# Three joints of a decoder stack: last output job, eviction, square, statistic, root, residual and first tile by halves of the tokens

## What is computed

```
for i in range(DEPTH_2):
    a = rms_norm_2(h, pre_mix_norm[i])
    m = hgrn2_mixer(...) if i == 0 else mla_mixer(...)     # ends in "@ w_out"
    h = h + rms_norm_2(m, post_mix_norm[i])                # joints "hg_post", "mla_post"
    f = squared_relu_mlp(rms_norm_2(h, pre_mlp_norm[i]), w_mlp_in[i], w_mlp_out[i])
    h = h + rms_norm_2(f, post_mlp_norm[i])
    e = p[i] @ w_ple_proj[i]
    g = sigmoid(h @ w_ple_gate[i])
    h = h + rms_norm_2(g * e, ple_norm[i])                 # joint "ple0_post" for i = 0
```

## Time and profile before

| | |
|---|---|
| median of 3 runs (lowest, highest) | 2754.61 us (2754.1, 2755.46) |
| the profiled execution: time, span | 2754.22 us, 2752.4 us |
| busy: PE, DVE, ACT, POOL | 2680.1, 1367.5, 1213.1, 1071.2 us |
| instructions: PE, DVE, ACT, POOL | 13878, 2435, 1883, 803 |
| mean granted TensorE clock | 0.994 |

### The profile page before, as it was taken

The page is one execution under the profiler, slowest core; times in us unless marked ns, Lnnn a source line. Parts: engine busy times, 40 slices in busy tenths (PEclk is TensorE's granted clock), DMA queues, the critical chain, the costliest instruction groups (busy, mean ns, idle before and its releaser), DMA issues.

```text
span 2752.4 us, 41868 instructions
## 1 busy us (share of the span) xinstructions
PE 2680.1 (97%) x13878; PEld 2137.5 (78%) x13878; DVE 1367.5 (50%) x2435; ACT 1213.1 (44%) x1883; POOL 1071.2 (39%) x803
## 2 busy tenths in 40 slices
PE   7999999999999999999999999999999999999999
PEld 6887777767777777778887788887677877788886
DVE  7335333676666567676755321128753353321126
ACT  5224433544444455565544432235554463433234
POOL 5544333423233333443344444444412213444442
PEclk9999999999999999999999999999999999999999
DMA  4332222211121221222223333333211202333331
GB/s 160 96 96 81 83 72 72 69 54 55 37 61 44 70 69 61 78 76 69 69 69 92 92 96 95 93 109 92 77 39 41 66 31 69 99 93 97 93 107 54
DMA packets 59641, 211.87 MB, mean 77 GB/s; under 512 B 6688, under 2 KB 7072, under 8 KB 59552
## 3 DMA queue, kind: packets, MB, share of 16 engines
q1 hardware_dynamic: 57744, 206.89, 24.6%
q10 hardware_dynamic: 1520, 2.75, 0.3%
q0 software_dynamic: 288, 1.05, 0.1%
HBM read 208.57 MB, written 2.10 MB: 77 GB/s over the span
## 4 chain that ended last, share of the span: by engine, by line
issue 36%; PE 23%; POOL 17%; DVE 2%; POOLq 0%; ACT 0%; DVEq 0%
POOL weights_low L374 17%; PE bank L1323 6%; PE bank L1325 6%; PE bank L1324 6%; PE bank L1427 2%; PE bank L1409 0%; PE bank L1450 0%; PE bank L1434 0%; DVE work L1761 0%; PE bank L1535 0%; DVE activations_low L454 0%; PE bank L1516 0%; PE bank L1540 0%; PE bank L1512 0%; DVE residual L2374 0%
## 5 line engine op out<-in xcount | busy, mean ns | idle before, releaser
L374 POOL TENSOR_TENSOR weights_low<-weights_raw,weights_high 128x512 fp32r<-128x512 f32 x776 | 1042.3, 1366 | 1539.4 <-ACT weights_high L358 1520.6
L1323 PE MATMUL bank<-activations_high,weights_high 128*128 128x512 f32 x2912 | 1184.4, 407 | 38.5 <-POOL weights_low L374 16.8
L1325 PE MATMUL bank<-activations_high,weights_low 128*128 128x512 f32 x2912 | 1141.4, 392 | 0.0
L1324 PE MATMUL bank<-activations_low,weights_high 128*128 128x512 f32 x2912 | 1140.6, 392 | 0.0
L1323 PEld LDWEIGHTS bank<-activations_high,weights_high 128*128 128x128 f32 x2912 | 550.0, 189 | 176.2 <-issue 20.1
L1325 PEld LDWEIGHTS bank<-activations_high,weights_low 128*128 128x128 f32 x2912 | 549.5, 189 | 117.2
L1324 PEld LDWEIGHTS bank<-activations_low,weights_high 128*128 128x128 f32 x2912 | 550.8, 189 | 110.0 <-issue 8.4
L358 ACT ACTIVATE weights_high<-weights_raw 128x1024 fp32r<-128x1024 f32 x384 | 404.0, 1053 | 302.3 <-PE bank L1325 294.8
L2864 DVE TENSOR_TENSOR mixed<-bank,mixed 128x512 f32 (+1 forms) x48 | 33.2, 692 | 193.9 <-PE bank L1325 193.9
L2808 ACT ACTIVATE to_split<-work 128x512 f32<-128x512 f32 x64 | 40.5, 632 | 184.0 <-DVE work L2850 184.0
L2850 DVE SCALAR_TENSOR_TENSOR work<-bank,rstd 128x512 f32<-128x512 f32 x64 | 44.2, 690 | 144.4 <-PE bank L1325 138.6
(11 more groups left out here) (452 smaller groups left out, 3272.9 us busy)
## 6 DMA issues: line engine op xcount, KB each, us to landing
weights_raw<-weights SPq DMA_DIRECT2D x388, 512.0 KB, 3.6
out_t<-residual SPq DMA_DIRECT2D x8, 256.0 KB, 2.1
residual<-x_t ACTq DMA_DIRECT2D x2, 512.0 KB, 7.1
residual<-x_t POOLq DMA_DIRECT2D x2, 512.0 KB, 9.9
work<-p_t ACTq DMA_DIRECT2D x2, 512.0 KB, 4.2
const<-consts SPq DMA_DIRECT2D x1, 713.0 KB, 12.6
const<-consts SPq DMA_DIRECT2D x1, 321.0 KB, 11.5
root<-positions ACTq DMA_DIRECT2D x1, 256.0 KB, 3.1
```

Of the source, the lines that this page charges most:

```text
L374: K.nc.gpsimd.tensor_tensor(K.w_lo[:, s, part], K.raw[:, s, part], K.w_hi[:, s, part].bitcast(F32), ALU.subtract).then_inc(K.job_sems["low ...
L1323: K.nc.tensor.matmul(dst, wh, K.act_hi[:, t, :], start=k == 0, stop=False)
L1324: K.nc.tensor.matmul(dst, wh, K.act_lo[:, t, :], start=False, stop=False)
L1325: ins = K.nc.tensor.matmul(dst, wl, K.act_hi[:, t, :], start=False, stop=k == len(tiles) - 1)
```

## The change

At the three joints, the eighth job of the output phase and what follows it up to the first tile of the next phase are cut in two halves of 256 tokens (`COLUMNS`).

* PE (`joint_pe`): 24 matmuls of 128x256 for the first half into bank 6, then 24 for the second into the job's own bank. Between the second half's matmuls stand the statistic's matmuls, also in halves (banks 7 and 5): the sum of six before its first tile, the square of tile 6 before its third, the first half of the square of tile 7 before its sixth; the second half of it comes after the job. Two filling matmuls end it, where there were one and four.
* DVE and ACT evict, square, take the root of and add half after half, with a semaphore `joint` of 7 steps a joint. The square of tile 7 is now DVE's in all three (`joint_square`); in `hg_out` and `mla_outb` it was ACT's.
* The last `weight_high` ahead, which waits for the eighth job, is moved: between the two roots in `hg` and `mla`, behind the first tile's high part in `ple0`.
* The first high and low part of the next activations are made in halves; the low part of tile 0 is now made before tile 1 is begun.

```diff
+def joint_pe(e, stage, c, tiles):
+    K, s, (n, _) = e.K, c % SLOTS, STAT_SIZE[stage]
+    last, mm, ones = FIRST_SQUARE[stage] + n - 1, e.K.nc.tensor.matmul, e.K.c("ones")[:, 0:P]
+    def piece(k, half):
+        t, cut, dst = tiles[k], COLUMNS[half], joint_bank(e, c, half)
+        wh, wl = K.w_hi[:, s, k * P:(k + 1) * P], K.w_lo[:, s, k * P:(k + 1) * P]
+        mm(dst, wh, K.act_hi[:, t, cut], start=k == 0, stop=False)
+        mm(dst, wh, K.act_lo[:, t, cut], start=False, stop=False)
+        return mm(dst, wl, K.act_hi[:, t, cut], start=False, stop=k == DT - 1)
+    def summed(half, src, start=False, stop=False):
+        cut = COLUMNS[half]
+        return mm(K.ps[JOINT_STAT_BANKS[half]][:, cut], ones, src[:, cut], start=start, stop=stop)
+    job_start(e, c, None, 1)
+    for k in range(DT):
+        if k == DT // 2:
+            second_half(e, c)
+        ins = piece(k, 0)
+    joint_signal(e, ins)
+    e.eng.wait_ge(K.sem("rstd_ready"), STAT_NO[stage])
+    e.eng.wait_ge(K.sem("square_used"), last - 1)
+    for half in range(2):
+        ins = summed(half, K.root, True)
+    ins.then_inc(K.sem("sum_ready"), 1)
+    for k in range(DT):
+        if k == 2:
+            e.eng.wait_ge(K.sem("square_ready"), last)
+            for half in range(2):
+                ins = summed(half, K.sq[:, (last - 1) % 2, :])
+            ins.then_inc(K.sem("square_used"), 1)
+        if k == 5:
+            joint_wait(e, stage, 3)
+            joint_signal(e, summed(0, K.sq[:, last % 2, :], False, True))
+        ins = piece(k, 1)
+    ins.then_inc(K.job_sems["done"], 1)
+    e.eng.wait_ge(K.sem("square_ready"), last + 1)
+    summed(1, K.sq[:, last % 2, :], False, True).then_inc(K.sem("square_used"), 1)
...
 def ahead_act(e, phase, done=0):
...
-            if n == DT - 1:
-                weight_high(e, c0 + DT + AHEAD)
-            square_tile(e, SUMMED_BY[phase], 0, n)
+            if n < DT - 1:
+                square_tile(e, stage, 0, n)
+        joint_root(e, stage, 0)
+        weight_high(e, c0 + DT + AHEAD)
+        joint_root(e, stage, 1)
...
+def post_act(e, step, split, tile0=0, col=None, squares=None, weight=None):
...
+    if joint:
+        joint_wait(e, step + "_post", 6)
+        joint_signal(e, K.nc.scalar.activation(K.act_hi[:, tile0, COLUMNS[0]], K.X[:, 0, COLUMNS[0]], ACT.Copy, scale=col(0)))
     for k in range(DT):
+        cut = COLUMNS[1] if joint and k == 0 else slice(0, S)
         e.eng.wait_ge(K.sem("x_ready"), X_DONE[step] - DT + k + 1)
...
+        if weight and k == 0:
+            weight_high(e, weight)
         if squares:
             square_of(e, squares, k, K.X[:, k, :])
...
+    if joint:
+        for half, cut in enumerate(COLUMNS):
+            if half == 0:
+                joint_wait(e, stage, 5)
+            else:
+                stat_vector(e, stage)
+            e.steps.step(v.scalar_tensor_tensor(K.M[:, 0, cut], K.M[:, 0, cut], K.col(weight, col0), K.rstd[:, cut],
+                                                ALU.mult, ALU.mult))
+            e.steps.wait()
+            ins = v.tensor_tensor(K.X[:, 0, cut], K.X[:, 0, cut], K.M[:, 0, cut], ALU.add)
+            if half == 0:
+                joint_signal(e, ins)
+            else:
+                ins.then_inc(K.sem("x_ready"), 1)
+        joint_wait(e, stage, 7)
+        low_first(COLUMNS[0])
+        e.eng.wait_ge(K.sem("split_high_done"), FIRST_SPLIT[split] + 1)
+        low_first(COLUMNS[1]).then_inc(K.sem("split_done"), 1)
...
 def ple_act(e, name, layer):
...
+        last = gate + DT - 1
+        joint_wait(e, name + "_post", 1)
+        joint_signal(e, act(K.M[:, DT - 1, COLUMNS[0]], joint_bank(e, last, 0), ACT.Sigmoid))
+        square(DT - 2)
+        job_wait(e, last)
+        act(K.M[:, DT - 1, COLUMNS[1]], joint_bank(e, last, 1), ACT.Sigmoid).then_inc(K.job_sems["bank"][last % SLOTS], 1)
+        K.nc.scalar.preload_act_table_set("natural_log_exp_and_others")
+        for half in range(2):
+            joint_root(e, name + "_post", half)
```

More of the change, by code:

```diff
@@ new lines, in joint_square, with joint_root @@
+def joint_square(e, stage, half):
+    K, last = e.K, FIRST_SQUARE[stage] + DT - 1
+    src, cut = K.M[:, DT - 1, :], COLUMNS[half]
+    ins = K.nc.vector.scalar_tensor_tensor(K.sq[:, last % 2, cut], src[:, cut], 1.0 / D, src[:, cut], ALU.mult, ALU.mult)
+    if half == 0:
+        joint_signal(e, ins)
+    else:
+        ins.then_inc(K.sem("square_ready"), 1)
+def joint_root(e, stage, half):
+    K, cut = e.K, COLUMNS[half]
+    if half == 0:
+        joint_wait(e, stage, 4)
+    else:
+        e.eng.wait_ge(K.sem("square_used"), FIRST_SQUARE[stage] + DT)
+    ins = inverse_root(e, K.rstd[:, cut], K.root[:, cut], K.ps[JOINT_STAT_BANKS[half]][:, cut])
+    if half == 0:
+        joint_signal(e, ins)
+    else:
+        ins.then_inc(K.sem("rstd_ready"), 1)
@@ L710, in out_pe, with out_joint_pe @@
                 job(e, c0 + r, i, tiles)
+def out_joint_pe(e, phase, split, stage, tiles=B_TILES, skip=0):
+    c0 = FIRST_JOB[phase]
+    job_with_waits(e, c0, None, tiles, split, skip)
+    for n in range(1, DT - 1):
+        job(e, c0 + n, None, tiles)
+    joint_pe(e, stage, c0 + DT - 1, tiles)
+    keep_busy(e, 2)
 HELD = DT - 1
@@ L2310, in out_m_dve, with evicted @@
         e.steps.wait()
-    if phase == "hg_out":
-        for n in range(DT):
+    if phase in SUMMED_BY:
+        stage, v = SUMMED_BY[phase], K.nc.vector
+        def evicted(n, half=None):
+            if half is None:
+                m, bank = K.M[:, n, :], bank_of(e, c0 + n)[:, :]
+            else:
+                m, bank = K.M[:, n, COLUMNS[half]], joint_bank(e, c0 + n, half)
+            return v.tensor_tensor(m, bank, m, ALU.add) if add else v.tensor_copy(m, bank)
+        for n in range(DT - 1):
             job_wait(e, c0 + n)
-            K.nc.vector.tensor_copy(K.M[:, n, :], bank_of(e, c0 + n)[:, :]).then_inc(count, 1)
+            evicted(n).then_inc(count, 1)
             e.eng.wait_ge(count, base + n + 1)
@@ L2484, in hg_pe @@
         job(e, c0 + r)
[L2485 to L2486 removed]
+    out_joint_pe(e, "hg_out", "hg_y", "hg_post")
 def hg_act(e):
@@ L2949, in ple_pe @@
     quad_by_halves(e, gate, name + "_h", B_TILES)
-    for r in range(4, DT):
+    for r in range(4, DT if nth else DT - 1):
         job(e, gate + r, None, B_TILES)
+    if not nth:
+        for use in ("e5", "e6", "e7"):
+            ring.wait_read(use, nth)
+        joint_pe(e, name + "_post", gate + DT - 1, B_TILES)
+        keep_busy(e, 2)
+        return
     ring.wait_read("e6", nth)
-    if not nth:
-        stat_tensor(e, name + "_post")
-        return
     for use in ("e5", "e7"):
@@ L2988, in square @@
         square_of(e, name + "_post", n, K.M[:, n, :])
-    for n in range(DT):
+    for n in range(DT if nth else DT - 1):
         job_wait(e, gate + n)
@@ L3163, in mla_pe @@
                 mla_pair_pe(e, b, ring, ident, trip, c, i, s)
-        out_pe(e, out, "mla_y", A_TILES, part * DT)
-    stat_tensor(e, "mla_post")
+        if part:
+            out_joint_pe(e, out, "mla_y", "mla_post", A_TILES, DT)
+        else:
+            out_pe(e, out, "mla_y", A_TILES)
 def mla_values(e, c, bank, first):
```

96 lines of the change are left out of this document (68 added, 28 removed).

## The result

| | before | after |
|---|---|---|
| median of runs, us | 2755.03 (2754.1 to 2757.08, 6 runs) | 2766.42 (2764.64 to 2768.3, 6 runs) |
| span of the profiled execution, us | 2752.4 | 2762.8 |
| mean granted clock | 0.994 | 0.992 |

A forecast was written before the change was run, and what follows sets the result against it. PE's waits for one chain at three joints, 26.4 us together, were taken as the most that can be won. Losses of 1.4 (hg, mla), 5.2 (ple0) and 3.2 (clock), 9.8 on 2754.22, gave 2764.0, range 2757 to 2769.

The forecast's parts named there:

- case A: All three joints: the forecast itself, 9.8 us slower, 2764.0 us; chance 0.5.
- case D: Joints: all four idle times and a second one in a row lose clock, with slow forms; 14 us, 2768; chance 0.15.
- hg and mla, the chain: PE resumes at T+14.1 (T: eighth job's first matmul), 0.5 us later than now, because POOL's instructions hold up DVE.
- hg and mla, the tiles behind: PE waits 0.2 us at tile 1, nothing more lost later; with the chain 0.7 us a joint, 1.4 together.
- ple0, the sum of six: PE idles 3.6 us mid-job for the late sum of six; resumes at T+17.7, 2.85 us later than before.
- ple0, tile 1: DVE, held up by POOL, ends tile 1's low part 5.2 us behind tile 0's; PE stops 2.3 us.
- a wait of over 2 us: Sign in ple0: PE waits over 2 us for tile 1's low part, with DVE instructions of 1.1 to 1.8 beside POOL.
- The clock: Behind four new idle times at the joints, two falls to half clock at 1.6 us each: 3.2 us, bounds 0 and 6.4.
- The sum: Whole kernel: 1.4 at hg and mla, 5.2 at ple0, 3.2 for the clock, 9.8 us slower.
- B: Clock stays up or falls once, or POOL slips between DVE's at hg and mla: 6.6 or 4.6 us, 2759 to 2762; chance 0.25.
- C's turning point: ple0: whether the sum of six is in `K.root` by T+2.9, 3.6 us earlier than the trace has it.
- C: Joints: the halves overlap as they are laid out; -1.4 us, 2752.8 us; chance 0.1.

The follow-up runs named there:

- experiment 5: Changed kernel, but at hg and mla the last weights' high part stands behind tile 0's high part, as in ple0: 2768.64 us, ratio 1.0049 to before.
- Experiment 3: Changed kernel plus four fillers before ple0's wait for the sum of six, and four instead of two behind each joint: 2764.35 us, ratio 1.0035 to before.
- experiment 9: Changed kernel with last job whole, tile 0 whole, four fillers, weights' high part ahead of the roots; halves only for eviction, square, statistic, root: 2753.2 us, ratio 0.9994.
- Experiment 4: Changed kernel, but in ple0 the second half's 24 matmuls directly follow the first's, with both halves' sums behind them: 2759.2 us, ratio 1.0015 to before.
- experiment 6: Experiment 4's kernel, with ple0's last weights' high part moved back before the table load: 2758.23 us, ratio 1.0014 to before.
- experiment 7: Experiment 6's kernel with four fillers instead of two behind each joint: 2756.47 us, ratio 1.0006 to before.
- experiments 1: Changed kernel with ple0_post as before, only hg_post and mla_post by halves: 2759.19 us, ratio 1.0019 to before.

## Why the prediction was right, and where it was not

The forecast was 2764.0 in a range of 2757 to 2769; the median is 2766.4. The mechanisms at the three joints are those of case A, named as likeliest; only the number of falls of the clock is that of case D. Step by step:

- **hg and mla, the chain.** Right. T+14.1 was forecast, T+13.87 measured; without POOL T+13.1 was forecast, and experiment 5 gave T+12.89. DVE's add and multiply beside POOL take 1.37 and 1.46. The first is 0.42 plus most of what POOL's first instruction had left (with 1.30 us for it, 1500.12 + 1.30 - 1500.38 = 1.04, of which 0.95 is seen). Of the two, only the multiply's 0.98 moved PE, as forecast.
- **hg and mla, the tiles behind.** This is the term that failed. I had "PE waits 0.2" and "nothing more is lost". Experiment 3 shows 0.3 at tile 1 and 0.5 at the last tile, 0.8 in all where the sum had 0.2; with the 0.3 by which PE resumes later (0.5 in the sum) that is 1.1 a joint where the sum had 0.7. The step was that each later tile takes DVE 2.53 and PE 2.72, so that PE, once stopped at tile 1, never meets DVE again. By that PE would reach the last tile 19 us behind the resumption. It does so after 17.13 in before and 17.14 in experiment 9, because `raw_quad` does not have four jobs take every tile in turn: it does so for the first six tiles (`EARLY` is `DT - 2`), and then the first job alone takes tile 6, 3 matmuls, and comes to tile 7. That is 75 matmuls instead of 84, and in both traces PE makes 75 steps from the one to the other. DVE was just in time there already. Its pace of 2.53 holds in experiment 3, so the 0.8 by which tile 1 is late stays to the end, and PE pays the rest of it at the last tile.
- **ple0, the sum of six.** Right. PE's wait is 3.47 where 3.6 was forecast, the resumption at full clock T+17.51 (experiment 3) where it was T+17.7. In after the second half of the job is late by 1.3 more (T+13.2 where T+11.93 was forecast), which is the half clock. Experiment 4 takes the wait out of the job, and PE resumes 5.75 earlier than in after: 2.64 that were lost against before, 1.84 that the halves behind the job now win, and 1.3 of clock.
- **ple0, tile 1.** Right in mechanism, but the sign did not show. Tile 1's low part ends 5.1 behind tile 0's (5.2 forecast). The wait for it is 2.10 where nothing hides it (2.3 forecast), and experiment 6 removes it by moving the weights' parts ahead. In after only 0.49 of it is seen, where I had named a wait of over 2 us as a sign, since half clock in tile 0 fills the rest: the stall and the fall were added up and in fact overlapped.
- **The clock.** The sum had two falls at 1.6, 3.2 in all; there are four at the joints, and they cost less each. At hg and mla one is worth 0.74 and 0.77 (after against experiment 3). At ple0 the one behind the sum's wait moves the resumption by 18.78 - 17.51 = 1.3. For ple0 without any fall there is only an estimate: experiment 3 resumes 4.48 later than experiment 4 and costs 5.58 more, so its fall behind tile 1's wait cost 1.10, and without it ple0 would be at 5.5. The clock is then 1.3 of the 6.74, and 2.8 at the three joints together. That this is near 3.2 is luck: twice the falls at less than half the price. The error was to add the clock to the tile waits as if they were apart: a slow PE and a PE that waits for DVE lose the same microseconds.
- **The sum.** 9.8 was forecast for the profiled execution and 10.4 found. Without the clock 6.6 was forecast, and 1.09 + 5.5 + 1.11 = 7.7 is what the traces give, with the estimate above in it; the clock's 2.8 instead of 3.2 takes some of the difference back. The stretches outside the joints, +1.6 and -1.6, cancel by chance.
- **The rivals.** B asked for the clock to stay up: it did not stay up, and with the falls gone at hg and mla (experiment 3) the kernel is still at 2764.35. B's 4.6 also needed POOL to slip between DVE's instructions, and POOL met them. D had all four idle times followed by a fall, at 14 us. Four falls are there, one of them behind the 1.79 at ple0 instead of the forecast stall, and the median lies between A's 2764 and D's 2768; D's price of 1.6 for each fall was too high. C's turning point was right in kind: with the sum of six out of the way (experiments 4, 6 and 7) ple0 resumes 1.8 earlier than before, and once POOL is moved its price is -1.06 (experiment 7; in experiment 6, with a fall of the clock behind the joint, it is -0.24).

The Trainium skill (SBUF — State Buffer, Who interferes with whom) has DVE and POOL exclude each other for whole instructions. The trace agrees: 1.37 and 1.46 where alone it is 0.42 and 0.48, one POOL instruction each, an added time that does not grow with DVE's own. POOL's two instructions take 2.75 at hg and 2.99 at ple0, and 2.58 in experiment 6, where DVE is idle for most of them. The prediction's check on the earlier trace rows was loose: POOL had 1899.30 + 1.74 - 1899.81 = 1.23 left there, not 1.09, which is only the 1.78 less the 0.69.

What the change wanted, an earlier resumption, is to be had, and as far as the runs go not by the halved job. At hg PE resumes at T+12.14 with the job whole and T+12.89 with it in halves, with POOL out of the way in the second and nearly so in the first. The halved job ends later, at T+8.03 in after (1498.61 + 0.28) against T+5.61, by the statistic's calls that stand in it, and its first half's early result is of no use: tile 0's last low part waits for the second half's root.

## What to carry to other kernels

Cut into halves the relay that lies behind the last matmul, where engines wait for each other; here that is worth some 2 us in the traces and is at the edge of what the times can tell. Leave whole the job ahead of it, whose cut won nothing at ple0. The tile behind it may stay whole too if the vector engine is what feeds the next phase: its halves bring PE back 0.6 us earlier at hg and lose 0.8 at later tiles. Before a matmul group is moved behind a statistic's wait in program order, look up when that statistic is ready: here a wait of 3.5 us for a statistic that had been needed only behind all work came to stand in front of half a job. And give the POOL work that a moved weight part releases a place in the vector engine's idle time: the same two instructions make PE wait for nothing (ple0 in experiment 6), for 1.0 us (hg in after) or for 2.1 (tile 1 in experiments 4 and 5), depending on which vector instructions they meet.

## What the runs showed that I had not expected

The same wait is followed by a fall of the clock in one execution and by none in another. At hg the same code with the same idle time of 2.31 us was followed by 3.4 us at 1.2 GHz in after and in experiments 1 and 6, and by none in experiment 4. The wait of 1.89 us behind mla's opening, 1.90 in before, was followed by a fall in after (window 2362.00 to 2365.40 at 0.55) and by none in before. I forecast from two waits, 2.08 without a fall and 2.18 with one, as if a line ran between them. These runs show none: 1.79 and 1.89 were followed by falls, and 2.31 was not always. What decides it is not shown. A fall costs 0.74 to 1.6 us by what stands behind it. In code that no kernel here changes, the stretch up to hg's T, the thirteen profiled executions differ by up to 5.4 us (T from 1490.19 to 1495.58), so the span of a single one says little about a change of this size; a joint's price, taken inside one trace, and the median of 11 runs, which tells about 0.1%, say more.
